# Layered decoder step on one core: sample work moved between attention units, and the first output weights split

## The reference, cut to what matters

```python
def _nsa_core(q, qpos, k_cmp, v_cmp, k_blk, v_blk, overlap, k_win, v_win, kwpos, gates):
    ...
    p_s = _masked_probs(s_s, mask_s[:, :, :, None, :])
    o_s = jnp.einsum('bqgrk,bgqkd->bqgrd', p_s.astype(vg.dtype), vg)
    ...
    p_w = _masked_probs(s_w, mask_w)
    o_w = jnp.einsum('bqgrk,bkgd->bqgrd', p_w.astype(v_win.dtype), v_win)
    return gates[..., 0:1] * o_c + gates[..., 1:2] * o_s + gates[..., 2:3] * o_w

def _merge(x, ya, za, yb, zb, g_mix, p_i, w_out_a, w_out_b, w_o, w_ple, w_ple_gate):
    br_a = jnp.einsum('btc,cd->btd', jax.nn.silu(za) * ya, w_out_a)
    br_b = jnp.einsum('btc,cd->btd', jax.nn.silu(zb) * yb, w_out_b)
    ...
```

## Time and profile before

| | |
|---|---|
| time before, median of 3 runs | 2438.48 us (2438.44 to 2440.83) |
| the profiled execution's own time | 2440.18 us |
| its span, first to last instruction | 2438.4 us |
| busy, share of the span | PE 97%, DVE 50%, ACT 40%, POOL 9% |
| mean granted clock of TensorE | 0.993 |

### The profile page before, as it was taken

How to read it: one execution, slowest core, us unless ns; L and a number is a source line. 1 busy time by engine, 2 the same in 40 slices (tenths; PEclk the granted TensorE clock), 3 DMA queues, 4 the chain that set the end, 5 groups by cost and what they waited for, 6 DMA issues and landing times.

```text
span 2438.4 us, 45717 instructions
## 1 busy us (share of the span) xinstructions
PE 2358.7 (97%) x18047; PEld 2065.0 (85%) x18047; DVE 1228.0 (50%) x2324; ACT 987.5 (40%) x2024; POOL 208.4 (9%) x349
## 2 busy tenths in 40 slices
PE   8999999999999999899989999999999999998998
PEld 8999999997788655589989999999977885555998
DVE  4444232546675566564454432224567656665544
ACT  4232223435564455532333221234446545554332
POOL 0000000000000233310000000000000002334000
PEclk9999999999999999999999999999999999999999
DMA  6343354707642677663234334547086318867530
GB/s 236 121 138 104 87 169 124 162 19 159 90 50 35 107 121 121 124 197 112 85 127 137 123 104 96 169 115 162 5 172 88 52 19 135 120 111 163 165 115 37
DMA packets 293309, 279.10 MB, mean 114 GB/s; under 512 B 92601, under 2 KB 281465, under 8 KB 291816
## 3 DMA queue, kind: packets, MB, share of 16 engines
q1 hardware_dynamic: 288680, 239.34, 44.9%
q0 software_dynamic: 4416, 36.85, 4.1%
HBM read 249.25 MB, written 43.53 MB: 120 GB/s over the span
## 4 chain that ended last, share of the span: by engine, by line
PE 88%; DVE 5%; ACT 3%; DMA 1%; issue 1%; SPq 1%; DVEq 0%; POOL 0%; ACTq 0%
PE ps L771 47%; PE ps L1016 13%; PE ps L942 7%; PE ps L1143 3%; PE ps L1167 3%; PE ps L1126 2%; PE ps L969 2%; DVE chL L2127 2%; PE ps L1265 2%; PE ps L1041 1%; ACT chH L1646 1%; DMA v_win<-in_state_win 1%; PE ps L1413 1%; SPq L569 1%; PE ps L1273 1%
## 5 line engine op out<-in xcount | busy, mean ns | idle before, releaser
L771 PE MATMUL ps<-hH,wH 128*128 128x272 f32 x2016 | 418.7, 289 | 8.4 <-DVE hL L1970 8.3
L771 PE MATMUL ps<-hH,wL 128*128 128x272 f32 x2016 | 420.4, 290 | 0.0
L405 DVE TENSOR_TENSOR wL<-w_raw,wH 128x2048 fp32r<-128x2048 f32 (+1 forms) x107 | 246.1, 2300 | 346.2 <-ACT wH L396 343.9
L771 PE MATMUL ps<-hL,wH 128*128 128x272 f32 x2016 | 417.4, 289 | 0.0
L771 PEld LDWEIGHTS ps<-hH,wH 128*128 128x128 f32 x2016 | 318.7, 189 | 10.2 <-issue 7.5
L771 PEld LDWEIGHTS ps<-hH,wL 128*128 128x128 f32 x2016 | 317.4, 189 | 0.0
L771 PEld LDWEIGHTS ps<-hL,wH 128*128 128x128 f32 x2016 | 317.4, 189 | 0.0
L2127 DVE TENSOR_TENSOR chL<-ps,chH 64x256 fp32r<-64x256 f32 x512 | 216.5, 423 | 158.9 <-ACT chH L1646 151.3
L1646 ACT ACTIVATE chH<-ps 64x256 fp32r<-64x256 f32 x512 | 206.8, 404 | 214.5 <-PE ps L1016 205.9
L396 ACT ACTIVATE wH<-w_raw 128x2048 fp32r<-128x2048 f32 (+1 forms) x107 | 204.8, 1914 | 97.3 <-PE ps L771 77.6
L741 POOL TENSOR_SCALAR pr<-pr,inv,zg 128x512 f32<-128x512 f32 (+3 forms) x256 | 153.0, 607 | 966.1 <-DVE inv L2317 966.1
(11 more groups left out here) (337 smaller groups left out, 4037.9 us busy)
## 6 DMA issues: line engine op xcount, KB each, us to landing
w_raw<-in_w_in SPq DMA_DIRECT2D x59, 1024.0 KB
craw<-in_cache_kv SPq DMA_DIRECT2D x256, 128.0 KB, 5.1
w_raw<-in_w_in SPq DMA_DIRECT2D x64, 256.0 KB
k_sel<-in_cache_kv SPq DMA_DIRECT2D x128, 128.0 KB, 5.5
v_sel<-in_cache_kv SPq DMA_DIRECT2D x128, 128.0 KB, 10.5
out_new_win_sample<-in_state_win POOLq DMA_DIRECT2D x16, 1016.0 KB, 6.1
w_raw<-in_w_out_a SPq DMA_DIRECT2D x8, 1024.0 KB
k_win<-in_state_win SPq DMA_DIRECT2D x16, 512.0 KB, 6.9
```

The source lines that it names most:

```text
L405: dve.tensor_tensor(block_part(wL, b), block_part(w_raw, b), block_part(wH, b).bitcast(F32), ALU.subtract).then_inc(w_lo, 1)
L771: last = nc.tensor.matmul(ps[:, bank + hf, 0:HALF], st, x[:, k, hf * HALF:(hf + 1) * HALF], start=k == 0 and w is wH and x is xH, stop=k = ...
```

## The change

The number of instructions on PE and POOL and their order stay as they are. Five things move:

1. SP: the values of pair 3 are loaded before `zbs`, and SP waits for `zbs` to have landed (`zb_back`) before it issues `load_ob(0)`.
2. ACT and DVE: `make_high` and `make_low` of block `B_OB` leave the sample step of m = 7. In their place two halves of 1024 columns each: ACT's `out_high` at the end of units 60 and 62, DVE's `out_low` at the end of units 62 and 63.
3. DVE: the three small operations on the sums and gates of a back pair go from `k` = 3 to `k` = 2 (`combine_gains`), and the first product into `sy` from `k` = 3 to `k` = 4 (`combine`).
4. DVE: at `k` = 6 of a block with a back pair, `inverses(i + 1)` and `turned(i)` are done first and `copy_turned` after them.
5. With 4, at unit 62 the product of the sample columns also stands behind `inverses(63)` and `turned(62)`.

```diff
-                sp.wait_ge(sa_kt, 48 * l + 48)
-                sp.dma_start(zbs[:], a["zb_keep"][l].rearrange("k p t -> p k t")).then_inc(zb_back, 16)
-                sp.wait_ge(s_fin, 4 * l + 3)
-                load_half(l, 3, numbers, 3, v_sel, v_win, s_v)
...
+                sp.wait_ge(s_fin, 4 * l + 3)
+                load_half(l, 3, numbers, 3, v_sel, v_win, s_v)
+                sp.wait_ge(sa_kt, 48 * l + 48)
+                sp.dma_start(zbs[:], a["zb_keep"][l].rearrange("k p t -> p k t")).then_inc(zb_back, 16)
+                sp.wait_ge(zb_back, 16 * l + 16)
                 load_ob(0)
...
-                    if front is None:
-                        act.wait_ge(sa_s, 12 * l + 12)
-                        make_high(act, l, B_OB)
...
+                def out_high(k):
+
+                    if k == 0:
+                        act.wait_ge(sa_s, 12 * l + 12)
+                        act.wait_ge(w_in_sem[B_OB % 2], 64 * (l * (NB // 2) + B_OB // 2 + 1))
+                    to, frm = wH[:, B_OB % 2, k:k + 4, 0:BW], w_raw[:, B_OB % 2, k:k + 4, 0:BW]
+                    if k:
+                        act.activation(to, frm, ACT.Copy).then_inc(w_hi, 1)
+                    else:
+                        act.activation(to, frm, ACT.Copy)
...
+                    if i in (UNITS - 4, UNITS - 2):
+                        out_high(2 * (i - UNITS + 4))
...
-                    if front is None:
-                        make_low(dve, l, B_OB)
...
+                def out_low(k):
+
+                    dve.wait_ge(w_hi, l * NB + B_OB + 1)
+                    to, frm, hi = (w[:, B_OB % 2, k:k + 4, 0:BW] for w in (wL, w_raw, wH))
...
-                    if i:
+                    if i and (k < 7 or back is None):
                         inverses(i)
                         turned(i - 1)
...
-                    if k == 3 and back is not None:
-                        combine_first(back, 6 + (mm + 1) % 2)
+                    if k == 2 and back is not None:
+                        combine_gains(back)
                     if k == 4 and back is not None:
-                        combine_rest(6 + (mm + 1) % 2)
+                        combine(back, 6 + (mm + 1) % 2)
...
                     if k == 6 and back is not None:
+                        inverses(i + 1)
+                        turned(i)
                         copy_turned(mm)
...
+                    if i >= UNITS - 2:
+                        out_low(4 * (i - UNITS + 2))
```

More of the change, by code:

```diff
@@ L2381, in sample_drop, with combine_gains @@
                     dve.drain()
-                def combine_first(pair, bank):
+                def combine_gains(pair):
                     c = 92 + 2 * (pair % 2)
@@ L2391, in combine_first, with combine @@
                     dve.tensor_tensor(small[:, 80:83], grow[:, pair, :], small[:, 76:79], ALU.mult)
+                def combine(pair, bank):
+                    dve.wait_ge(sa_yt, 4 * l + pair)
                     dve.drain()
-                    dve.wait_ge(sa_yt, 4 * l + pair)
                     dve.tensor_scalar(sy[:], ps[:, bank, 0:P], small[:, 80:81], None, ALU.mult)
-                def combine_rest(bank):
                     for n in (1, 2):
@@ L2457, in sample_step @@
                         dve.tensor_tensor(swsc[:, 0:WIN], ps[:, 1, :], C("wmask"), ALU.add).then_inc(sa_se, 1)
+                def out_low(k):
+                    dve.wait_ge(w_hi, l * NB + B_OB + 1)
+                    to, frm, hi = (w[:, B_OB % 2, k:k + 4, 0:BW] for w in (wL, w_raw, wH))
+                    if k:
+                        dve.tensor_tensor(to, frm, hi.bitcast(F32), ALU.subtract).then_inc(w_lo, 1)
+                    else:
+                        dve.tensor_tensor(to, frm, hi.bitcast(F32), ALU.subtract)
                 def sample_bias(pair, br, s):
```

## The result

The changed kernel takes 2447.56 us (median of 7 runs, 2445.78 to 2449.41) against 2438.44 us (7 runs, 2436.86 to 2440.83) for the kernel before on the same chip: ratio 1.0037, 95% interval 1.0026 to 1.0049. It is 9.1 us slower. The forecast was 2436.9 us with a range up to 2444.5 us, so the time lies outside the range, on the side to which the forecast gave 0.12. The profiled execution took 2449.41 us, its span 2447.6 us at a mean granted clock of 0.988 (before: 2438.4 us and 0.993).

What follows compares the result with a forecast made beforehand. PE, busy 97% of the span, was taken as the bound, with gains only from its waits or clock. −3.9 − 1.6 + 3.3 + 3.0 − 2.4 = −1.6 us on 2438.48 gave 2436.9 us, range 2430.5 to 2444.5.

Steps and rivals of the forecast that it cites:

- step 1: Last sample step (m = 7): with values loaded ahead of `zbs`, PE's wait of 4.62 and 3.37 us for them goes.
- Rival D: Last sample step: values still land 15 us after issue, only the tail's cost and back-pair gains stay; +1.9 us, 2440.4; chance 0.03.
- rival C: At `turn(58)`: late `zbs` lengthens PE's 2.9 us stand until the clock falls; +4.4 us, 2442.9, up to 2445; chance 0.19.
- step 2: At `turn(58)`: `zbs` lands late, POOL's products bound it, PE stands 2.9 us; 3.9 and 1.6 us earlier in the two layers.
- step 5: Back pairs at `k` = 3, 4 and 6: DVE's new order saves 0.6 us each, four times, 2.4 us earlier.
- step 3: SP's queue: waiting for `zb_back` before the output weights costs nothing, with some 6 us of cover for `load_ob(0)`.
- step 4: End of attention: moved split of `B_OB` delays the last `output` to +15.3 us from `turn(58)`; 3.3 and 3.0 us later.
- rival B: At `turn(58)`: `zbs` lands early enough that PE sets the time; 8.6 us faster, 2429.9, with half of it 2433; chance 0.18.
- T: Experiments' theory, both PE stands: forecast mechanisms act as worked out, but the clock falls to 0.50 behind each, the loss.
- R: Experiments' rival theory: the moved work itself (transfers, POOL's products, split on ACT and DVE) is the loss; the clock only follows.

Runs made afterwards that it cites:

- p345: Kernel before with only the new DVE order in blocks with a back pair (gains, product, `copy_turned`, unit 62): 2438.22 us, ratio 0.9996 to the kernel before.
- fill58: Changed kernel with 32 useless identity matmuls on PE ahead of its wait for POOL at `turn(58)`: 2451.37 us, ratio 1.005 to the kernel before.
- fill16: Changed kernel with 16 useless identity matmuls on PE ahead of its wait for POOL at `turn(58)`: 2443.44 us, ratio 1.002 to the kernel before.
- nowait: Changed kernel without SP's wait for `zbs` to land before it issues the output weights: 2450.17 us, ratio 1.0044 to the kernel before.
- sp: Kernel before with only SP's list changed (values ahead of `zbs`, wait for `zbs` before the output weights): 2448.1 us, ratio 1.0036 to the kernel before.
- ahead: Changed kernel with DVE's `turned(63)` moved ahead of its two split pieces and first `bL`: 2440.10 us, ratio 1.0004 to the kernel before.
- spread: Changed kernel with POOL's seven `zbs` products dealt out behind the scalings of units 58 to 63: 2439.64 us, ratio 1.0002 to the kernel before.
- spread_ahead: Same as `spread`, with DVE's `turned(63)` also ahead of its `zbs` product and both split pieces: 2433.91 us, ratio 0.998 to the kernel before.
- tail: Kernel before with only the split of `B_OB` moved, in halves, to units 60 to 63: 2443.49 us, ratio 1.0018 to the kernel before.
- spread2: Same as `spread_ahead`, with POOL's products one unit earlier (two behind unit 57, one behind each of 58 to 62): 2430.03 us, ratio 0.9961 to the kernel before.

## Why the prediction was wrong

**The values' wait (step 1).** Right. No wait for `v_win`, 64 matmuls in 1.96 us (forecast 2.1). The last transfers of the values landed 6.5 and 9.2 us after their issue, so by 1020.8 at the latest, 22.1 us after the first issue against 21.3 in the forecast. The rule of the Trainium skill (DMA: Bandwidth & Descriptors, section on queues, rings and completion order), that each DMA engine takes its descriptors in ring order, let the forecast say that `zbs` behind the values does not hold them: the trace agrees. Rival D is out.

**"At 2.9 I say it does not"** (rival C). This is the step that failed, and the costliest. The forecast put two stands of PE in its own sum, 2.9 us at `turn(58)` and some 3 us ahead of the last `output`, and put the clock behind both at nothing. The clock fell behind both in both layers. Behind 3.00 us ahead of the last `output` it is 0.50, which the forecast gave half a sentence ("could do the same"), and `p345` shows it behind 2.37 us. The price in the trace: 17.63 − 15.10 = 2.5 us for the units behind `turn(58)` in the first layer and 17.46 − 15.14 = 2.3 in the second (15.10 from `fill58`, 15.14 from `fill16`), 0.9 on each last `output`, and 0.4 and 1.5 on the chunks of the output tile. That is 8.5 of the 10.8 us between the forecast's −1.6 and the spans' +9.2.

**`zbs` late next (step 2).** That POOL bounds `turn(58)` was right. That POOL starts at 1027.03 (forecast 1027.3) and `turn(58)` at 1036.97 (1037.3) is luck: two errors meet. The values were issued 1.5 us earlier than in the sum of step 2, by the gains of step 5, and from that issue to POOL's start 28.3 and 28.5 us passed in the two layers, against 27.1. The forecast took 6.0 us for the bytes of `zbs` and 0.8 for their landing behind the last byte of the values, and that was too little. Counted from the issue, `turn(58)` comes 2.8 and 0.3 us earlier than before, not 3.9 and 1.6.

The stand was too short in "1025.5 + 8.9 = 1034.4. So POOL bounds it, and PE stands 2.9 us." The 8.9 is confirmed by 8.68 (from 1023.81 to 1036.97 − 4.48 = 1032.49). But the step begins at 1023.81. It is 2.2 us ahead at the start of the sample step (L1217 at 1021.23, L1216 before at 1023.47): 1.5 us from m = 2 and 4, which move the transfers too and leave the stand as it is, and 0.75 from m = 6, which lies behind the issue and lengthens the stand. Of the 1.6 us by which the stand outgrew the forecast, 1.2 are the later `zbs` and 0.4 are PE's side. So PE stood 4.48 and 4.63 us, beyond even the 3.37 us after which rival C let the clock fall.

**SP's wait on `zb_back` (step 3).** Its zero was right for the whole change: `nowait`, without it, is no faster. In `sp`, where the split stood where it was, the later weights made part 1 cost 9.0 us.

**The split at the end (step 4).** Forecast +15.3 us from `turn(58)` to the last `output` at full clock; `fill58` gives 15.10 and `fill16` 15.15. The hand count of the order was right to 0.2 us. What it cost in the kernel was 21.60 − 15.07 = 6.5 us up to the second chunk in place of 3.3, and 21.42 − 15.42 = 6.0 in place of 3.0. The 3.2 us more in the first layer are the 2.5 and 0.9 of clock named above, less the 0.2 of the count.

**The back pairs (step 5).** 0.75 us for each of m = 2 and 4 (1.5 us up to the issue of pair 3's values) against 0.6, within its bounds. At `turn(58)` the longer way of `zbs` had taken 1.2 of these 1.5 us again. `output` at `k` = 4 comes 0.92 us earlier in its block (forecast 0.95), with 0.21 us of stand left; new waits of 0.49 and 0.25 us stand at `k` = 5, and none at `k` = 7, as said.

**The sum** then reads, with `turn(58)` as the mark: first layer −4.3 (forecast −5.1 with the back pairs), up to the second chunk +6.5 (+3.3), the slow clock behind it +0.4 (0), between the layers +0.8 (0), second layer −1.8 (−2.8), +6.0 (+3.0) and +1.5 (0): 9.2 us, but for rounding. The 0.8 us between the layers hold a wait of PE of 1.08 us for the cached rows (`craw`) at 1820.09 that the kernel before does not have. The traces of `fill16`, `ahead` and `nowait` show no such step there, so it looks like chance in this one execution; its cause is open. One slip in the forecast's own working: half of rival B's 8.6 us gives 2434.2, not 2433.

T is shown for both places: filling either stand with useless work wins 4.1 and 5.9 us. Doing the same work in another order wins 7.9 us with the first stand gone (`spread`), 7.5 us with the second nearly gone (`ahead`) and 13.7 us with both moves (`spread_ahead`), where a slow stretch at the end remains. R keeps one part: about 3 us a layer of DVE's own late work at the end are real and come back only with its order.

## What to carry to other kernels

A wait of TensorE has two prices, the wait and the clock behind it. Here the second was 2.5 and 2.3 us behind stands of 4.48 and 4.63, and 1.3 and 2.5 us behind stands of 3.00. So a change that makes a forecast stand of PE must be summed with the slow stretch behind it. A gain ahead of a transfer's issue moves the transfer too and is kept; a gain between the issue and the place that the transfer bounds only lengthens the stand there. When a late product keeps PE waiting, deal it out between the small operations that PE needs (here POOL's seven products of 1.23 us), and put the copy that PE waits for ahead of everything that it needs later.

## What the runs showed of the hardware

- The clock fell behind stands shorter than the 3.37 us known before: behind 3.00 us in the changed kernel, 2.37 and 1.60 us in `p345`, and where short stands follow each other 1.76, 1.01 and 0.47 (`tail`) and 1.33, 0.59 and 1.71 (`spread2`). In `spread` it fell half a microsecond into a stand, with one of 1.33 us shortly before. It did not fall in `ahead` behind 0.99, 0.60 and 1.70. So the length of the single stand does not decide it, and no row here gives the border.
- DVE's product of 256 columns took 1.51 us beside POOL's products and 0.43 without them, its piece of 1024 columns 2.28 and 1.22. What was added is nearly the same for both sizes, 1.08 and 1.06 us, and less than the 1.27 us of one of POOL's products there; so the factor says little for another size. Both have two inputs in SBUF, and the Trainium skill (GPSIMD Engine Reference, Specifications) says that POOL's interface to SBUF is shared with DVE, with contention for such instructions: the trace agrees. An instruction of 128x2 with one input, 0.16 us otherwise, also took 1.07 and 1.30 us beside POOL's products in the changed kernel, in a stretch that those products bounded in any case:

```profile
1034.35 1.30 DVE L2326 TENSOR_SCALAR sums<-sums 128x2 f32<-128x2 f32 x1
```

- 2.2 MB of `zbs`, which move in 6.0 us at the rate of the earlier trace rows, took 14.7 and 15.0 us from issue to landing behind the values in the same queue, and 16.0 and 15.6 us with the weights issued right behind them.
